# Rows without the norm's root, convolution taps of two tiles begun early, and another order of routing, in a two-layer decoder trunk

## The chip, the cores and the metric

The kernel runs on one core of a Trainium2 chip. The metric is the device time of one execution in microseconds (us), from 3 runs. A core has four engines for arithmetic, each with its own stream of instructions that runs strictly in the order written: TensorE (matrix products, PE in the rows), VectorE (DVE), ScalarE (ACT) and GpSimd (POOL). SyncE (SP) only starts transfers (DMAs) here. Engines wait for each other through semaphores. PSUM is the memory into which TensorE writes, 8 banks of 512 f32 for each of 128 partitions; SBUF is the memory of the others' tiles and of the weights.

## What is computed

272 rows (16 meta tokens ahead of 256) of 1024 values pass two layers, each a mixer and a feed-forward part, all in float32. The RMS norm stands ahead of each of the four; the diff touches the second and the third, and the routing of the fourth.

```python
def rms_norm(x, g):
    y = xf * lax.rsqrt(jnp.mean(xf * xf, axis=-1, keepdims=True) + EPS)
    return y * g

# layer 0: h = h + conv_sb_mixer(h); h = h + swiglu(rms_norm(h, ffn_norm_even), ...)
#   mixer: u = silu(layer_norm(causal_depthwise_conv(a * sigmoid(gate), width 31)))  (512 channels)
#          o = stick_breaking attention, 8 heads of 64; concat(u, o) @ w_out
def swiglu(x, w_gate, w_up, w_down):            # 1024 -> 2688 -> 1024
    return (jax.nn.silu(x @ w_gate) * (x @ w_up)) @ w_down

# layer 1, mixer (1408 channels)
    hcat = rms_norm(x, norm_g) @ w_in
    gate, xb = jnp.split(hcat, 2, axis=-1)
    gate = jax.nn.gelu(gate, approximate=True)
    xb = causal_depthwise_conv(xb, conv_w, conv_b)            # width 4
    # r, i = sigmoid(block-diagonal products of xb + bias)
    # a = exp(-8 r softplus(-lambda)); y_t = a y_(t-1) + sqrt(1 - a^2) i xb
    return (gate * y) @ w_out
# layer 1, experts: softmax over the top 2 of 8 logits, each expert a swiglu 1024 -> 3584 -> 1024
```

## The kernel before

**Layout.** Activations lie turned: channels on the partitions, the 272 rows along the free dimension, so `h` is 8 tiles (KD) of 128 x 272. The weights stream through in numbered *units* of 128 x 2048 f32 (1 MB; the last of a matrix may be smaller), and a unit is the step of the whole first part of the program: 0 to 3 the convolution's inputs (`U_CONV`), 4 to 9 q, k and v, 10 and 11 diagonal taps, 12 to 15 the even mixer's output (`U_OUT_E`), 16 to 37 the FFN's gate and up products in turn (`U_FFN1`), 38 to 49 its down projection (`U_FFN2`), 50 to 55 the odd mixer's input (`U_IN_O`), 56 to 61 its block-diagonal gates (`U_BAND`), 62 to 67 its gelu branch (`U_GELU`), 68 to 73 its output (`U_OUT_O`), and from 74 (`U_MOE`) on the experts, 84 units for each. The odd mixer has KL = 11 tiles of channels, in pairs with one alone at the end; its T of 272 columns are SEQ = 256 in the gelu branch.

**One product in three.** A float32 product is made of three at TensorE's rounded float32 (`three`, line 1529): each operand is split in a high part and the rest. For a weight unit ScalarE writes `whi` (line 639) and VectorE `raw_lo` = raw - `whi` (line 1010); the activations have pairs `hn_hi`/`hn_lo` (normalised rows), `hid_hi`/`hid_lo` (FFN), `xb_hi`/`xb_lo` (odd mixer). `raw` has 7 buffers, `whi` 6, and the experts' weights 14 (`MOE_RAW`).

**What sets the order.** ScalarE and VectorE each walk the units: split of unit u + 2 (u + 4 from `U_BAND` on, `AHEAD`), then `after(u)`, the work that hangs on unit u's products. So what VectorE does behind unit u stands behind the split of a later unit. TensorE's `features(u, ...)` does the products of unit u into PSUM banks `pair(u)` = 2 (u mod 3) and the next one.

**A norm** between two parts has this chain: VectorE adds the residual (line 1075 or 1099), ScalarE squares pairs of tiles (`square_pair`), TensorE sums the squares over the partitions with a product by ones (`norm_sums`, line 1552, bank 7), ScalarE takes the root as exp(-0.5 ln x) (`inverse_root`, into `rs`), then `norm_low` on VectorE and `norm_high` on ScalarE form h x gain x root, split, tile by tile. The next unit's first product needs the first tile, so TensorE waits for the whole chain after the last sums.

**FFN.** Behind each up unit ScalarE takes silu of the gate's bank (line 717), VectorE multiplies it by the up bank (`fh`, line 1087), ScalarE copies the high part and VectorE subtracts (line 1091). The down projection waits for the eleventh of these before its first product.

**Attention.** Heads go two at a time: scores, a log of 1 + exp, sums over later keys on TensorE, exp, product with v. Between VectorE's steps of it (`ll` line 1148, `zm` line 1176) stand the depthwise convolution's taps, `conv(n)` (line 1046), n at a time: tile by tile of `cacc`, each waiting for the tap before. Three of the four channel tiles (`CONV_PE`), 31 taps each, are done so; TensorE does the fourth, and parts of others, with diagonal matrices.

**Odd mixer.** Behind each input unit ScalarE writes the first tap from PSUM into `xc` (line 735), VectorE adds three more, again from PSUM (`lru_conv`, line 1239), and both split `xb`. Then ScalarE forms gates from `U_BAND`'s products. From `U_GELU` on VectorE scans (`scan(m)`, lines 1253 to 1258, the tiles of `SCAN_AT`), multiplies by the gelu (`gated`, line 1261) that ScalarE has made from PSUM (line 766), and subtracts the high part of the result (`y_low`, line 1265) that ScalarE copied (`y_high`). The gelu units' banks are `gelu_bank` = 0, 2, 4, 0, 2, 0, so the fourth unit may start once the first gelu is done, and the sixth once the fourth is. `turn_residual` brings `h` to the layout of rows in the first units of the input.

**Routing and experts.** TensorE gives the output in rows, VectorE adds `h_tok` in two halves (`acc`, line 1297), TensorE turns `acc` for the router's product (line 1777), the other two copy it out, VectorE picks the two best experts (`choose`), ScalarE sums the squares for the fourth norm, VectorE scales (`xs`, line 1321). The counts of earlier rows for each expert come from three small products, then rows are gathered with selection matrices `sel_m` (line 1806) and the experts follow. SyncE starts the experts' weight transfers in pieces of `over_gates_raw` (line 570), the first once the odd mixer's last low part stands, since they take the room of its tiles.

## Time and profile before

| | us |
|---|---|
| median of 3 runs | 1410.21 |
| lowest, highest | 1408.6, 1413.44 |
| the profiled execution's own time | 1408.68 |
| its span | 1406.7 |
| TensorE busy in it | 1334.8 (95%) |
| VectorE, ScalarE busy | 775.8 (55%), 639.3 (45%) |
| mean granted clock of TensorE | 0.977 |

TensorE's 95% is an average over two stages that differ. Up to some 540 us it works on the two layers' dense parts with other engines in turn; behind that the experts' weights come in at about 400 GB/s, and matrix products and transfers run side by side. Two lines of the page, busy share and transfers in 40 slices of 35 us, let the reader see the border at the sixteenth slice. The chain of work that ended last is 72% TensorE, 7% DMA, 5% VectorE and 4% ScalarE.

### The profile page before, as it was taken

The page shows a single profiled execution, that of the slowest core. Times are in us where ns is not written, and L with a number is a line of the kernel's source. Part 1 is how long each engine was busy: PE and PEld are TensorE (multiplying, and loading weights), DVE is VectorE, ACT ScalarE, POOL GpSimd, SP SyncE. Part 2 cuts the span into 40 slices and gives each one's busy share as a digit, 9 for nine tenths or more (in the row PEclk, how much of TensorE's full clock was granted, in tenths as well). Part 3 has the DMA queues.
Part 4 walks back from the last instruction along what each step waited for, and adds up shares of the span by engine and source line. Part 5 has one row for each costly group of instructions (what it writes and reads, how often), then busy time and mean ns, then how long its engine had stood idle before and what let it go on. Part 6 is the DMA issues. An engine that isn't in the chain of part 4 may idle for free.

```text
span 1406.7 us, 18570 instructions
## 1 busy us (share of the span) xinstructions
PE 1334.8 (95%) x7469; PEld 1011.3 (72%) x7469; DVE 775.8 (55%) x781; ACT 639.3 (45%) x581; POOL 19.1 (1%) x16
## 2 busy tenths in 40 slices
PE   6988889999999999999999999999999999999997
PEld 6977789999998978887336887345888335788433
DVE  5787455544476777994106984105995104987101
ACT  5453444433358756773006873005874004875100
POOL 0001000000002000000000000000000000000000
PEclk9997999999999998999999999999999999999999
DMA  9330245554526469998999999999999999999995
GB/s 329 105 106 30 65 141 170 156 167 158 182 90 189 165 234 385 364 363 326 396 410 409 412 409 410 391 408 411 412 407 412 412 407 412 412 406 413 406 406 234
DMA packets 149572, 426.34 MB, mean 303 GB/s; under 512 B 7664, under 2 KB 65648, under 8 KB 135152
## 3 DMA queue, kind: packets, MB, share of 16 engines
q1 hardware_dynamic: 149488, 425.12, 79.6%
q8 instruction: 65, 1.06, 0.3%
q14 instruction: 19, 0.16, 0.0%
HBM read 424.04 MB, written 1.05 MB: 302 GB/s over the span
## 4 chain that ended last, share of the span: by engine, by line
PE 72%; DMA 7%; DVE 5%; ACT 4%; issue 2%; SPq 1%; DVEq 0%; ACTq 0%
PE P L1529 51%; PE P L1919 12%; DMA over_gates_raw<-in_moe_w_gate 5%; PE P L1943 3%; PE P L1806 2%; DVE raw_lo L1010 1%; SPq L570 1%; DMA raw<-in_moe_w_down 1%; PE P L1827 1%; PE P L1861 1%; ACT whi L639 1%; ACT whi L867 1%; PE P L1552 0%; DVE over_gates_lo L1285 0%; PE P L1824 0%
## 5 line engine op out<-in xcount | busy, mean ns | idle before, releaser
L1529 PE MATMUL P<-hn_hi,whi 128*128 128x272 f32 (+1 forms) x640 | 187.6, 293 | 14.6 <-DVE hn_lo L1031 12.6
L1285 DVE TENSOR_TENSOR raw_lo<-raw,whi 128x2048 fp32r<-128x2048 f32 x84 | 189.3, 2287 | 10.7 <-ACT whi L867 10.1
L1529 PE MATMUL P<-hn_hi,raw_lo 128*128 128x272 f32 (+1 forms) x640 | 186.1, 291 | 0.0
L1529 PE MATMUL P<-whi,xe_hi 128*128 128x512 f32 x448 | 179.2, 400 | 7.1 <-DVE over_gates_lo L1285 7.1
L1529 PE MATMUL P<-hn_lo,whi 128*128 128x272 f32 (+1 forms) x640 | 185.7, 290 | 0.0
L867 ACT ACTIVATE whi<-raw 128x2048 fp32r<-128x2048 f32 x84 | 160.9, 1918 | 53.8 <-PE P L1529 33.0
L1010 DVE TENSOR_TENSOR raw_lo<-raw,whi 128x2048 fp32r<-128x2048 f32 (+3 forms) x72 | 149.9, 2105 | 53.7 <-ACT whi L639 53.7
L1529 PE MATMUL P<-whi,xe_lo 128*128 128x512 f32 x448 | 177.4, 396 | 0.0
L1285 DVE TENSOR_TENSOR over_gates_lo<-over_gates_raw,whi 128x2048 fp32r<-128x2048 f32 x72 | 162.9, 2287 | 19.4 <-ACT whi L867 18.8
L867 ACT ACTIVATE whi<-over_gates_raw 128x2048 fp32r<-128x2048 f32 x72 | 137.4, 1917 | 42.9 <-PE P L1529 17.3
L1529 PEld LDWEIGHTS P<-hn_hi,whi 128*128 128x128 f32 x640 | 122.5, 191 | 16.6 <-issue 13.8
L1504 DVE TENSOR_TENSOR hb<-silu,P 128x512 f32<-128x512 f32 (+1 forms) x16 | 9.9, 621 | 220.2 <-PE P L1919 220.2
L639 ACT ACTIVATE whi<-raw 128x2048 fp32r<-128x2048 f32 (+3 forms) x72 | 124.3, 1757 | 2.6 <-DMA raw<-in_w_in_even 2.6
L1529 PEld LDWEIGHTS P<-hn_lo,whi 128*128 128x128 f32 x640 | 123.0, 192 | 0.0
L1529 PEld LDWEIGHTS P<-hn_hi,raw_lo 128*128 128x128 f32 x640 | 122.7, 192 | 0.0
L1919 PE MATMUL P<-raw,xe_f 128*64 128x512 f32 (+1 forms) x576 | 114.8, 548 | 0.0
L1529 PEld LDWEIGHTS P<-whi,xe_hi 128*128 128x128 f32 x448 | 84.7, 189 | 31.4 <-DVE over_gates_lo L1285 11.3
L968 ACT ACTIVATE silu<-P 128x512 f32<-128x512 f32 (+1 forms) x16 | 8.7, 544 | 205.0 <-PE P L1919 205.0
L1529 PE MATMUL P<-raw_lo,xe_hi 128*128 128x512 f32 x256 | 101.2, 395 | 0.0
L1529 PEld LDWEIGHTS P<-whi,xe_lo 128*128 128x128 f32 x448 | 84.5, 189 | 19.1
L1529 PE MATMUL P<-whi,ht_lo 128*128 128x512 f32 x224 | 88.7, 396 | 0.0
L1529 PE MATMUL P<-whi,ht_hi 128*128 128x512 f32 x224 | 88.4, 395 | 0.0
(284 smaller groups left out, 2072.2 us busy)
## 6 DMA issues: line engine op xcount, KB each, us to landing
raw<-in_moe_w_up SPq DMA_DIRECT2D x64, 1024.0 KB, 15.1
raw<-in_moe_w_gate SPq DMA_DIRECT2D x64, 1024.0 KB, 15.2
over_gates_raw<-in_moe_w_down SPq DMA_DIRECT2D x64, 1024.0 KB, 16.6
over_gates_raw<-in_moe_w_gate SPq DMA_DIRECT2D x48, 1024.0 KB, 18.8
raw<-in_moe_w_down SPq DMA_DIRECT2D x40, 1024.0 KB, 15.5
over_gates_raw<-in_moe_w_up SPq DMA_DIRECT2D x32, 1024.0 KB, 16.3
over_xb_raw<-in_moe_w_up SPq DMA_DIRECT2D x16, 1024.0 KB, 15.2
raw<-in_w_in_even SPq DMA_DIRECT2D x10, 1024.0 KB, 10.6
```

Of the source, the lines that this page charges most:

```text
L570: sp.dma_start(moe_raw[k % MOE_RAW][:, :].rearrange("p (k m) -> p k m", k=kk), src)\
L639: act.activation(whi[u % HI][:, 0:w], raw[u % RAW][:, 0:w], ACT.Copy).then_inc(hi_ready, 1)
L867: act.activation(whi[u % HI][:, :], moe_raw[k % MOE_RAW][:, :], ACT.Copy).then_inc(hi_ready, 1)
L1010: dve.tensor_tensor(lo(u)[:, 0:w], raw[u % RAW][:, 0:w], whi[u % HI][:, 0:w].bitcast(F32), ALU.subtract).then_inc(lo_ready, 1)
L1285: dve.tensor_tensor(moe_lo(k), moe_raw[k % MOE_RAW][:, :], whi[u % HI][:, :].bitcast(F32), ALU.subtract).then_inc(lo_ready, 1)
L1504: dve.tensor_tensor(hb[:, 0:n], silu[:, 0:n], small_up(s), ALU.mult).then_inc(h_ready, 1)
L1529: last = pe.matmul(dst, lhs, rhs, start=start and n == 0, stop=stop and n == 2)
L1806: last = pe.matmul(P[:, 6 + k // 4, 128 * (k % 4):128 * (k % 4) + n], xs[:, c, 128 * k:128 * k + 128], sel_m[:, c, 0:n], start=c == 0, sto ...
L1827: last = pe.matmul(P[:, scatter_bank(n), :], sel_t[:, tokens], ys[:, 512 * half:512 * half + 512], start=True, stop=True)
L1861: last = pe.matmul(turn_banks(s)[:, 128 * n:128 * n + 128], tile_of(hb, n), cst("ident"), is_transpose=True, start=True, stop=True)
L1919: last = pe.matmul(dst[HALVES[b]], xe_f[:, k], w[:, at:at + half], start=k == 0, stop=k == KD - 1)
L1943: last = pe.matmul(P[HALVES[b], 4, :], ht_f[:, x:x + SMALL], w[:, at:at + 512], start=s == 0 and n == 0, stop=s == STEPS - 1 and n == tile ...
```

## The change

The diff has three parts.

**Convolution taps.** `conv` no longer goes through the taps of all three tiles in step, but by a list, `CONV_ORDER`: the first 12 taps of tiles 0 and 1 first, then the first 24 of tile 2 between the next 12 of both, then the rest. Eight taps are done behind each of units 1 to 3, ahead of q; behind each of the units from q on it is 10 (was 9), and between attention's steps 6 (was 10), as long as taps are left. `CONV_PER_UNIT` and `CONV_PER_PAIR` are the numbers.

**Rows without the root.** For the FFN and the odd mixer's input and gelu branch, `hn_hi`/`hn_lo` are now h x gain, without the root: ScalarE writes the high part and VectorE (`late_low`) the low part of each pair of tiles as soon as the residual is added. The sums of the last pair of squares are taken inside the first unit of the next part (`sums`), and the root (`late_root`) is formed while TensorE does that unit. The results are multiplied by the root, one factor per row (`by_token`): VectorE scales the gate's and the up's bank (`fgs`, `fh`) ahead of silu, the input's bank into a new tile `xn` from which the taps now read, and the gelu branch's bank into `gg` (`gelu_input`), where ScalarE takes the gelu in place. A bank is free once it is scaled. `gated` moves behind the two scans. The down projection waits for ten of the eleven parts of `hid`, in other banks (`down_bank`), and for the eleventh at its second group.

**Routing.** ScalarE's squares of each row block move ahead of copies, `choose(0)` moves behind the inverse, one of the splits of the experts' weights moves from ahead of the adds to ahead of the subtraction for the gathered rows, and the counts over all rows go to bank 5 with a signal of their own.

```diff
-CONV_PER_UNIT, CONV_PER_PAIR = 9, 10
+CONV_EARLY, CONV_PER_UNIT, CONV_PER_PAIR = 8, 10, 6
...
+CONV_ORDER = [(s, c) for s in range(12) for c in range(2)]
...
+CONV_ORDER += [(s, c) for s in range(24, CONV_W) for c in range(CONV_PE)]
...
+        def by_token(n, cols=slice(0, T)):
+
...
+        def down_bank(c):
+            return 2 * ((c + 2) % 3)
...
+                    for k in (2 * c, 2 * c + 1):
+                        last = act.activation(hn_hi[:, k], h[:, k], ACT.Copy, scale=v(NORMS[n], k))
+                    last.then_inc(nhi_ready, 1)
...
+            def late_root(n):
+
+                act.wait_ge(ss_ready, n + 1)
+                inverse_root(rs[:, 0], P[:, 7, 0:T], D, root_ready)
...
-                    act.wait_ge(unit_used, u)
+                    act.wait_ge(ffn_scaled, j + 1)
...
-                    act.activation(fsg[:, 0:n], P[:, pair(u - 1):pair(u - 1) + n, 0:T], ACT.Silu).then_inc(ffn_silu, 1)
...
-                    act.wait_ge(unit_used, u + 1)
+                    act.wait_ge(xn_ready, j + 1)
...
+                        act.wait_ge(gelu_scaled, g + 1)
+                        act.activation(gg[:, 2 * g:2 * g + n], gg[:, 2 * g:2 * g + n], ACT.Gelu_apprx_tanh)\
...
+            def squares(c):
+                act.wait_ge(h2_ready, c + 1)
...
+            squares(0)
             act.wait_ge(xt_done, 2)
             act.activation(*turned_copy(0, None), ACT.Copy).then_inc(xt_act, 1)
+            squares(1)
...
+                dve.wait_ge(nhi_ready, 4 * n + c + 1)
+                for k in (2 * c, 2 * c + 1):
+                    last = dve.scalar_tensor_tensor(out=hn_lo[:, k], in0=h[:, k], scalar=v(NORMS[n], k),
+                                                    in1=hn_hi[:, k].bitcast(F32), op0=ALU.mult, op1=ALU.subtract)
+                last.then_inc(norm_ready, 1)
...
-                    s, c = x // CONV_PE, x % CONV_PE
+                    s, c = CONV_ORDER[x]
...
+                    dve.wait_ge(uin_ready, c + 1)
+                    conv(CONV_EARLY)
+                elif u == 2:
+                    conv(CONV_EARLY)
...
+                    if u > U_OUT_E:
+                        late_low(1, u - U_OUT_E - 1)
...
                     dve.wait_ge(unit_used, u + 1)
...
+                    dve.tensor_tensor(fgs[:, 0:n], P[:, pair(u - 1):pair(u - 1) + n, 0:T], by_token(n), ALU.mult)\
+                        .then_inc(ffn_scaled, 1)
+                    dve.tensor_tensor(fh[:, 0:n], P[:, pair(u):pair(u) + n, 0:T], by_token(n), ALU.mult)\
+                        .then_inc(ffn_up, 1)
...
-                    if j >= 1:
-                        dve.wait_ge(ffn_lo, j)
...
+                    dve.tensor_tensor(fh[:, 0:n], fsg[:, 0:n], fh[:, 0:n], ALU.mult).then_inc(ffn_h, 1)
...
+                    if c >= 1:
+                        late_low(2, c - 1)
...
-                            gated(m)
+                        gelu_input(g)
...
+                    if 0 <= g < len(BAND_UNITS):
+                        for m in BAND_UNITS[g]:
+                            gated(m)
...
+                dve.wait_ge(unit_used, u + 1)
+                dve.wait_ge(root_ready, 3)
...
+                dve.tensor_tensor(xn[:, 0:n], P[:, xb_bank(j):xb_bank(j) + n, 0:T], by_token(n), ALU.mult)\
+                    .then_inc(xn_ready, 1)
...
-                        dve.scalar_tensor_tensor(out=xc[:, m, s:T], in0=P[:, xb_bank(j) + t, 0:T - s],
+                        dve.scalar_tensor_tensor(out=xc[:, m, s:T], in0=xn[:, t, 0:T - s],
...
+            def gelu_input(g):
+                n = min(2, KL - 2 * g)
+                dve.wait_ge(unit_used, U_GELU + g + 1)
...
+                dve.tensor_tensor(gg[:, 2 * g:2 * g + n], P[:, gelu_bank(g):gelu_bank(g) + n, 0:SEQ],
+                                  by_token(n, slice(META, T)), ALU.mult).then_inc(gelu_scaled, 1)
...
-            choose(0)
             dve.wait_ge(h2_sq, 2)
             inverse(st[:, 4:6], st[:, 0:2], D, h2_inv, 0)
+            choose(0)
...
+                dve.wait_ge(counted, 1)
+                step(dve.tensor_copy(count[:, :], P[:, 5, 0:NE]))
...
+            split_item_lo((0, 0), READY_LO - 2)
...
-            for k in range(READY_LO - 1, READY_LO):
-                split_item_lo((0, 0), k)
+            split_item_lo((0, 0), READY_LO - 1)
...
+                    if sums is not None and m == 0:
+                        norm_sums(sums, 3)
...
-            norm_sums(1, 3)
...
                     pe.wait_ge(ffn_h, (u - 3 - U_FFN1) // 2 + 1)
...
+                    pe.wait_ge(added_e, u - U_FFN1 + 2)
...
+                features(u, hn_hi, hn_lo, pair(u), norm=first, sums=first)
...
                 if u == U_FFN2:
+                    pe.wait_ge(ffn_h, (KF + 1) // 2 - 1)
+                if c == 1 and part == 0:
                     pe.wait_ge(ffn_h, (KF + 1) // 2)
...
-                features(u, hid_hi, hid_lo, 2 * (c % 3), k0=8 * part, start=part == 0, stop=part == 2)
+                features(u, hid_hi, hid_lo, down_bank(c), k0=8 * part, start=part == 0, stop=part == 2)
...
-            norm_sums(2, 3)
...
-                    pe.wait_ge(gelu_ready, n - 2 if n < 5 else 4)
+                    pe.wait_ge(gelu_scaled, n - 2 if n < 5 else 4)
...
+            pe.matmul(P[:, 4, NE:2 * NE], cst("tri_lt"), chosen[:, 1], start=False, stop=True).then_inc(slots_done, 1)
...
+            pe.matmul(P[:, 5, 0:NE], ones[:, :], chosen[:, 1], start=False, stop=True).then_inc(counted, 1)
```

What the three parts do to the order, at three places. First VectorE inside attention: `cacc` is the convolution's accumulator (its last number is the columns left after the shift), `ll` and `zm` are the steps of a pair of heads, `raw_lo` a split of weights. Before, from the second of two `ll`:

```order
L1148 SCALAR_TENSOR_TENSOR ll<-zm,lx 128x864 [waits zm_ready,ln_ready]
L1150 TENSOR_TENSOR ll<-ll,con 128x864 [waits dve_step]
L1046 SCALAR_TENSOR_TENSOR cacc<-uin,vec,cacc 128x251 [waits conv_step] x2
...
L1046 SCALAR_TENSOR_TENSOR cacc<-uin,vec,cacc 128x248 [waits conv_step] x2
L1010 TENSOR_TENSOR raw_lo_61<-raw_54,whi_63 128x2048 [waits hi_ready]
L1176 TENSOR_TENSOR zm<-P,zm 128x864 [waits r_done]
L1137 SCALAR_TENSOR_TENSOR zm<-P,con 128x432 [waits wexp_ready,z_done]
...
L1148 SCALAR_TENSOR_TENSOR ll<-zm,lx 128x864 [waits r_done,zm_ready,ln_ready]
...
L1046 SCALAR_TENSOR_TENSOR cacc<-uin,vec,cacc 128x247 [waits conv_step] x3
...
L1046 SCALAR_TENSOR_TENSOR cacc<-uin,vec,cacc 128x245 [waits conv_step] x3
L1176 TENSOR_TENSOR zm<-P,zm 128x864 [waits r_done]
```

After, from the last tap ahead of the first `ll` on:

```order
L1080 SCALAR_TENSOR_TENSOR cacc<-uin,vec,cacc 128x243 [waits conv_step] x3
L1194 SCALAR_TENSOR_TENSOR ll<-zm,lx 128x864 [waits zm_ready,ln_ready]
...
L1194 SCALAR_TENSOR_TENSOR ll<-zm,lx 128x864 [waits zm_ready,ln_ready]
...
L1080 SCALAR_TENSOR_TENSOR cacc<-uin,vec,cacc 128x242 [waits conv_step] x3
L1036 TENSOR_TENSOR raw_lo_61<-raw_54,whi_63 128x2048 [waits hi_ready]
L1222 TENSOR_TENSOR zm<-P,zm 128x864 [waits r_done]
L1183 SCALAR_TENSOR_TENSOR zm<-P,con 128x432 [waits wexp_ready,z_done]
...
L1194 SCALAR_TENSOR_TENSOR ll<-zm,lx 128x864 [waits r_done,zm_ready,ln_ready]
...
L1222 TENSOR_TENSOR zm<-P,zm 128x864 [waits r_done]
L1183 SCALAR_TENSOR_TENSOR zm<-P,con 128x432 [waits wexp_ready,z_done]
...
L1194 SCALAR_TENSOR_TENSOR ll<-zm,lx 128x864 [waits r_done,zm_ready,ln_ready]
```

The taps between the second `ll` and the first `zm` of the links (10) have become 3, and ahead of the next `zm` there are none; the tap list had got to its end.

Second, VectorE from the even output's last units to the first of the FFN: `h` is the residual add, `scr` the row times gain and root, `hn_lo` the low part of the row. Before:

```order
L1075 TENSOR_TENSOR h<-P,h 128x544 [waits unit_used]
L1010 TENSOR_TENSOR raw_lo_59<-raw_52,whi_68 128x2048 [waits hi_ready]
L1075 TENSOR_TENSOR h<-P,h 128x544 [waits unit_used]
L1025 SCALAR_TENSOR_TENSOR scr<-h,vec,rs 128x272 [waits root_ready,added_e]
...
L1031 TENSOR_TENSOR hn_lo<-scr,hn_hi 128x544 [waits nhi_ready,nf_ready]
...
L1010 TENSOR_TENSOR raw_lo_60<-raw_53,whi_63 128x2048 [waits hi_ready]
L1010 TENSOR_TENSOR raw_lo_61<-raw_54,whi_64 128x2048 [waits hi_ready]
L1087 TENSOR_TENSOR fh<-fsg,P 128x544 [waits ffn_silu,unit_used]
L1091 TENSOR_TENSOR hid_lo<-fh,hid_hi 128x544 [waits ffn_hi,ffn_h]
L1010 TENSOR_TENSOR raw_lo_62<-raw_55,whi_65 128x2048 [waits hi_ready]
```

After:

```order
L1036 TENSOR_TENSOR raw_lo_59<-raw_52,whi_68 128x2048 [waits hi_ready]
L1111 TENSOR_TENSOR h<-P,h 128x544 [waits unit_used]
L1064 SCALAR_TENSOR_TENSOR hn_lo<-h,vec,hn_hi 128x272 [waits nhi_ready]
...
L1064 SCALAR_TENSOR_TENSOR hn_lo<-h,vec,hn_hi 128x272 [waits nhi_ready]
...
L1036 TENSOR_TENSOR raw_lo_61<-raw_54,whi_64 128x2048 [waits hi_ready]
L1125 TENSOR_TENSOR fgs<-P,rs 128x544 [waits root_ready,unit_used]
L1127 TENSOR_TENSOR fh<-P,rs 128x544
L1131 TENSOR_TENSOR fh<-fsg,fh 128x544 [waits ffn_silu,ffn_up]
L1134 TENSOR_TENSOR hid_lo<-fh,hid_hi 128x544 [waits ffn_hi,ffn_h]
L1036 TENSOR_TENSOR raw_lo_62<-raw_55,whi_65 128x2048 [waits hi_ready]
```

The low parts stand behind each add and wait for ScalarE's high part alone, not for the root; the root is waited for by the first scaling, `fgs`.

Third, the gelu branch. VectorE before, one round (`tt<-tt,gg` is `gated`, `xb_lo` is `y_low`, the pieces between belong to the scans of two tiles):

```order
L1010 TENSOR_TENSOR raw_lo_61<-raw_54,whi_65 128x2048 [waits hi_ready]
L1261 TENSOR_TENSOR tt<-tt,gg 128x256 [waits gelu_ready,scanned] x2
L1265 TENSOR_TENSOR xb_lo<-tt,xb_hi 128x256 [waits y_hi_ready] x2
L1253 SCALAR_TENSOR_TENSOR tt<-rg,tt 128x272 [waits bscale_ready,decay_ready,xi_ready]
...
L1256 SCALAR_TENSOR_TENSOR tt<-rg,ig 128x272 [waits dve_step]
L1010 TENSOR_TENSOR raw_lo_62<-raw_55,whi_66 128x2048 [waits hi_ready]
```

After:

```order
L1036 TENSOR_TENSOR raw_lo_61<-raw_54,whi_65 128x2048 [waits hi_ready]
L1317 TENSOR_TENSOR gg<-P,rs 128x512 [waits unit_used]
L1327 TENSOR_TENSOR xb_lo<-tt,xb_hi 128x256 [waits y_hi_ready] x2
L1307 SCALAR_TENSOR_TENSOR tt<-rg,tt 128x272 [waits bscale_ready,decay_ready,xi_ready]
...
L1310 SCALAR_TENSOR_TENSOR tt<-rg,ig 128x272 [waits dve_step]
L1323 TENSOR_TENSOR tt<-tt,gg 128x256 [waits gelu_ready,scanned] x2
L1036 TENSOR_TENSOR raw_lo_62<-raw_55,whi_66 128x2048 [waits hi_ready]
```

And ScalarE there, after (before, the same places read `gg<-P` with a wait for `unit_used`):

```order
L789 ACTIVATE gg<-gg 128x512 [waits gelu_scaled]
L861 ACTIVATE xb_hi<-tt 128x256 [waits y_ready] x2
L656 ACTIVATE whi_65<-raw_54 128x2048 [waits raw_full5,unit_used]
L789 ACTIVATE gg<-gg 128x512 [waits gelu_scaled]
```

The scaling stands ahead of `y_low` in VectorE's round, and in ScalarE's the gelu of the scaled tile stands ahead of the high part that `y_low` waits for; `gated` comes a whole round of scans after the gelu.

## Rows read from the trace of the kernel before

**Rows 1.** Chain of waits in order of time (start us, length us, what)

```profile
663.72 7.02 PE P L1919 x32
...
750.69 11.38 PE P L1529 x48
...
966.96 11.36 PE P L1529 x48
```

**Rows 2.** The page's slices, what the transfers moved in each fortieth of the span

```profile
GB/s 329 105 106 30 65 141 170 156 167 158 182 90 189 165 234 385 364 363 326 396 410 409 412 409 410 391 408 411 412 407 412 412 407 412 412 406 413 406 406 234
```

**Rows 3.** Timeline (start us, length us, engine, line, operation, sizes, [idle before and releaser])

```profile
505.71 2.23 SPq L570 DMA_DIRECT2D over_gates_raw<-in_moe_w_gate  x4
...
520.03 2.35 DVE L1297 TENSOR_TENSOR acc<-P,h_tok 128x1024 f32<-128x1024 f32 x2
...
529.96 2.48 DVE L1321 SCALAR_TENSOR_TENSOR xs<-acc,st,gain 128x1024 f32<-128x1024 f32 x2
...
533.18 6.42 PE L1806 MATMUL P<-sel_m,xs 128*128 128x128 f32 x32 [1.21 <-DVE sel_m L1336]
```

**Rows 4.** Timeline of TensorE at the named holes

```profile
317.24 0.39 PE L1529 MATMUL P<-hid_hi,whi 128*128 128x272 f32 x1 [2.17 <-DVE fh L1087]
...
472.78 0.39 PE L1529 MATMUL P<-hn_hi,whi 128*128 128x256 f32 x1 [0.99 <-ACT gg L766]
...
521.39 3.48 PE L1777 MATMUL P<-con,acc 128*128 128x128 f32 x16 [3.00 <-DVE acc L1297]
```

**Rows 5.** Timeline of VectorE in attention

```profile
121.56 1.05 DVE L1176 TENSOR_TENSOR zm<-P,zm 128x864 f32<-128x864 f32 x1
...
130.41 3.52 DVE L1046 SCALAR_TENSOR_TENSOR cacc<-uin,vec,cacc 128x244 f32<-128x244 f32 x9
...
136.05 1.05 DVE L1176 TENSOR_TENSOR zm<-P,zm 128x864 f32<-128x864 f32 x1
```

**Rows 6.** The FFN's and the odd norm: two links of the chain, then the timeline

```profile
166.61 0.92 PE P L1552 x4
...
167.53 6.02 PE P L1529 x48
```

```profile
180.53 0.72 DVE L1075 TENSOR_TENSOR h<-P,h 128x544 f32<-128x544 f32 x1 [1.39 <-PE P L1529]
...
194.84 0.63 ACT L717 ACTIVATE fsg<-P 128x544 f32<-128x544 f32 x1 [0.25 <-PE P L1529]
...
383.60 0.72 DVE L1099 TENSOR_TENSOR h<-P,h 128x544 f32<-128x544 f32 x1 [7.83 <-PE P L1529]
...
398.68 1.05 ACT L735 ACTIVATE xc<-P,vec 128x272 f32<-128x272 f32 x2 [4.14 <-PE P L1529]
```

**Rows 7.** Timeline of VectorE, the eleventh part of the hidden rows

```profile
309.10 0.72 DVE L1087 TENSOR_TENSOR fh<-fsg,P 128x544 f32<-128x544 f32 x1 [7.27 <-PE P L1529]
```

**Rows 8.** Windows: us, busy PE PEld DVE ACT POOL, PEclk, DMA share, GB/s

```profile
105.00:110.00 5.00, 5.00 (x23) 4.87 (x22) 5.00 (x9) 0.00 (x0) 0.00 (x0) 0.50 0.00 0
...
390.00:398.00 8.00, 8.00 (x45) 7.95 (x46) 5.70 (x8) 3.11 (x3) 0.00 (x0) 0.67 0.00 0
```

**Rows 9.** Timeline of VectorE, taps of the odd mixer

```profile
425.58 2.52 DVE L1239 SCALAR_TENSOR_TENSOR xc<-P,vec,xc 128x271 f32<-128x271 f32 x6 [1.45 <-ACT xc L735]
...
430.32 1.56 DVE L1239 SCALAR_TENSOR_TENSOR xc<-P,vec,xc 128x271 f32<-128x271 f32 x3
```

**Rows 10.** Timeline of ScalarE and VectorE in the gelu branch

```profile
472.13 0.60 ACT L766 ACTIVATE gg<-P 128x512 f32<-128x512 f32 x1
...
473.55 0.75 DVE L1261 TENSOR_TENSOR tt<-tt,gg 128x256 f32<-128x256 f32 x2
...
482.98 2.27 DVE L1010 TENSOR_TENSOR raw_lo<-raw,whi 128x2048 fp32r<-128x2048 f32 x1
...
485.83 0.75 DVE L1265 TENSOR_TENSOR xb_lo<-tt,xb_hi 128x256 fp32r<-128x256 f32 x2
...
489.66 2.27 DVE L1010 TENSOR_TENSOR raw_lo<-raw,whi 128x2048 fp32r<-128x2048 f32 x1
```

97 lines of the change are left out of this document (53 added, 44 removed).

## Prediction

> **What bounds the kernel now.** I read the chain of waits in order of time first, then TensorE's own waits, then the other engines' rows around each of them. The end of the program is the expert stage: the second and the third pair of experts start 216.3 us apart (750.69 and 966.96 [rows 1]) while the transfers move some 410 GB/s in slice after slice [rows 2]. So the stage from 540 us on is a stream of weights at the transfers' rate, and no edit of the change touches it. What it can do is start earlier. Its start has two parts: the first expert transfer, which SyncE issues at 505.71 when the last low part of the odd mixer's result stands, and TensorE's first expert product, which follows the gather of 533.18 + 6.42 = 539.60 [rows 3]. The first 56 chunks (42 of the first expert and 14 of ring) need 56 x 2.57 us (216.3 / 84 chunks) = 144 us, so they would be in by 652 us; the first small expert begins at 663.72 [rows 1]. The transfers thus have some 12 us of slack against TensorE's start, and the end moves with TensorE's start as long as the first transfer does not fall back by more than that. Everything below is the shift of that start.
>
> Before it, TensorE is the bound, with named holes: 2.17 us ahead of the down projection, 0.99 in the gate products, 3.00 before the transposes of routing [rows 4], those inside attention, and the two norms.
>
> **Convolution taps.** 93 taps on VectorE, 39 of them inside attention, 10 ahead of each of three links of the chain and 9 ahead of the fourth. Now 24 run under the first input units (VectorE idles there) and 9 are left in attention: 6, then 3. A tap costs 3.52 / 9 = 0.39 us [rows 5]. One tap more ahead of attention costs 0.4. The first `ll` then starts 1.1 us earlier, TensorE's sums too; behind them stand 45 products of the diagonal taps, so the next link (121.56) gains only 2.4 us: TensorE is late there, no longer VectorE. The link at 136.05 loses its 9 taps as well: 2.4 + 3.4 = 5.8 us [rows 5]. All behind it hangs on it: **-5.8**, between -2.4 (if only TensorE's part counts) and -7.
>
> **FFN norm.** Unit 15 ends as VectorE adds at 180.53; the first FFN unit ends as ScalarE reads it at 194.84 [rows 6]: 14.3 us. A unit takes 6.02, a pair of norm sums 0.92. The rows without the root need only the add (0.72), ScalarE's two products (some 0.8) and VectorE's two (0.9): ready 2.5 us after the unit, while TensorE has 0.92 of sums and 2.3 of products of the first six tiles. So 0.92 + 6.02 + 0.92 = 7.9 with the last sums inside, and the root (Ln, Exp) has 12 us until the first scaling. 14.3 - 7.9 = 6.4; I take **-6.2**. Some 1.9 of it are the clock: that first unit took 7.9 us behind the wait, not 6.02. Low end -4.3.
>
> The price of the root comes back on every pair of FFN units: two more VectorE multiplies of 0.72 and a silu that can't begin before the up unit ends. From that end: scale gate, then silu beside scale up, multiply = 2.3 us to `ffn_h`, 2.9 to the high part; TensorE asks for the bank at 6.0. Cover: one unit. VectorE's load rises from 5.9 to 7.4 of 12 us. Nothing, unless the chain more than doubles.
>
> **Down projection.** It waited 2.17 us for `ffn_h` 11 behind two splits. It now asks for 10, in banks that are free. But its own low part is late: unit 35 ends at 309.10 [rows 7]; 2.9 us of chain, 1.9 of split by ScalarE, 2.3 by VectorE give 316.2 against 317.24: **-1.1**, from -2.2 to 0.
>
> **Odd norm and input.** 383.60 to 398.68 [rows 6] is 15.1 us; now 6.02 + 0.92 + some 0.35 waiting for the last pair = 7.3: -7.7, of which 2.7 is the clock (0.67 granted in 390 to 398 [rows 8]: the 1.2 GHz level for two thirds, after a wait). Then part is given back. Per unit VectorE now does split 2.2, scale 0.7, wait for ScalarE's first tap 0.45, `xb_lo` 0.7, six taps 2.44 = 6.5 us against TensorE's 6.02, and it starts 2 us late, since the split of unit 52 waits on ScalarE behind the root. Stepped through the six units, the last tap ends 35.2 us after the first unit where it was 33.2 (431.88 - 398.64) [rows 9]. ScalarE's gates hang on that, and its chain is the bound until the scans: +2.0. Together **-5.7**, between -7.7 and -3.7.
> A rule speaks for the better end: the Trainium skill (Perfetto Trace Analysis, Optimizing Scalar/DVE Operations) gives VectorE about 60 ns of overhead on SBUF and 125 on PSUM, and these taps now read `xn` in SBUF; an estimate by it is 33 x 0.065 = 2.1 us back, and a sum of -11.1. The rows show none of it: six taps from PSUM over 270 columns take 0.42 us each [rows 9], nine from SBUF over 243 take 0.39 [rows 5], and the 27 columns account for that. I stay with the rows.
>
> **Gelu and the output: the loss.** Here VectorE, not TensorE, is the chain: one round of 6.68 us (482.98 to 489.66) is split 2.2, `gated` 0.67, `y_low` 0.67, two scans 3.16 [rows 10]. The change puts the scaling (0.63 each, six of them) into it. Worse, the order: ScalarE's gelu waits for the scaling, the high part of y stands behind gelu on ScalarE, and VectorE's next instruction is the low part of it. From the scaling's start: 0.69, 0.5 of the gelu's 0.6 until ScalarE issues the next, 0.4, so `y_low` starts at 1.65 and not at 0.63: 1.02 us idle a round. Round: 8.33. TensorE's last gate unit needs the fourth scaling (it needed the fourth gelu, long done). From the same 471.36: first scaling at 473.55, second 479.1, third 487.5, fourth 495.8, done 496.5. TensorE has unit 65 from 474.3, 66 until 485.85, and starts 67 at 496.5 instead of 484.4 (472.78 [rows 4] and two units of 5.8): **+12.1** on all that follows. Its rows there are otherwise gapless, so nothing takes it back. The hole of 10.6 us also drops the clock; behind the norms' holes 1.9 and 2.7 were lost, I take **+2**. The first transfer moves by +8.2 only, so the slack holds. Ends: +6 (were the idle hidden and the clock kept) and +19.
>
> **Routing.** VectorE adds `acc` at 520.03, 1.6 us after TensorE's end, behind the third split; that split moves, and the first half is added before that end, so the transposes start 3.0 us earlier. The squares (2 x 1.2) move ahead of the copies, the copies of row block 1 end 3.9 us after TensorE's end (was 6.3), the two choices follow the root, and `xs` (2.48) [rows 3] ends at 9.8 instead of 14.05; gather at 10.5 instead of 14.8: **-4.3**, between -7 (with the gather at full clock, 3.5 instead of 6.42) and -2. Counting in bank 5 is off the path.
>
> **Sum**: -5.8 - 6.2 - 1.1 - 5.7 + 12.1 + 2 - 4.3 = **-9.0 us**. The profiled run took 1408.68 (span 1406.7 plus 2.0), the median is 1410.21: 1399.7 or 1401.2, I say 1400.5.
>
> **Rivals.**
> 1. The gelu round costs only its instructions (ScalarE's order hides the idle, the clock holds): 3 x 1.02 + 2 less, -14, so 1396. For it: ScalarE has time to spare there, 0.6 us of gelu a round. Against: the order is strict on both engines. 0.12.
> 2. The holes cost more and attention gives less: the low clock lasts as long as behind the hole before 101.48, where it still was 0.50 in 105 to 110 [rows 8], some 10 us, 5 lost instead of 2, and attention only -2.4: -2.6, 1407.5, no difference. 0.13.
> 3. The clock part of the norms does not come back, the low level falls elsewhere: without 1.9, 2.7 and 2 the sum is -6.4, so 1404. Beside it stands the Trainium skill (TensorE: Matmul & The Clock Gate, Part 1), which puts the ramp under 1% of a typical span and advises against fitting it; 0.05, the rows [rows 8] show it.
> 4. Slower: behind the 10.6 us hole TensorE stays at the low level through the output products. 132 products at 0.235 are 31 us, as much again if all are at half rate: -9.0 - 2 + 31 = +20, 1430. It decides from 22 us at the low level on. Against: behind the norm's hole it came back under work, inside 390 to 398. 0.04.
>
> **How the numbers follow.** Forecast 0.66 (1396.5 to 1405), rivals as given. A measurement of this kernel tells 0.3% (4.2 us) from nothing: faster needs under 1406. Faster 0.66 + 0.12 + 0.05, less 0.01 for the forecast's own tail: 0.82; same 0.13 + 0.01; slower 0.04. The range takes in rivals 1 to 3 and the worse ends of attention and odd input: 1393 to 1408.
>
> **What would show it.** After's TensorE waits: none over 0.5 us at either norm, about 1 at the down projection, about 10 before one gate unit on the gelu scaling; the first FFN unit in 6 us; the clock low right behind that hole; the first expert product at about 530.5 and the first transfer at about 495. It is wrong if the last gate unit waits under 5 us, if FFN units wait at all, or if the first expert product moves and the end does not.

## The result and the profile after

The changed kernel takes 1398.92 us (median of 5 runs, 1393.68 to 1402.48), the kernel before 1411.84 over the five runs that stand beside them: a ratio on record of 0.9919, with an interval of 0.9898 to 0.9940 (the quotient of the two medians is 0.9909). The forecast was 1400.5, between 1393 and 1408. The span of the profiled execution went from 1406.7 to 1397.1 us, by 9.6, where the sum on record had 9.0.

Two sums that agree prove little: five of the seven terms hold within 0.5 us, two are off by 1.8 and 1.6 us in opposite directions, and one of the five, the routing, has its size only beside another term. The rows first.

The experts' stage, from the chain of waits (start us, us, what), as [rows 1]:

```profile
530.23 22.23 PE P L1592 x96
...
741.23 11.36 PE P L1592 x48
...
957.30 11.36 PE P L1592 x48
```

The pairs still stand 216.1 us apart, and each of these starts is 9.4 to 9.7 us earlier than its like in [rows 1] and the gather's end in [rows 3]. So the stage is moved as a whole and, but for 0.3 us, not changed, and everything that the change did lies ahead of 530 us.

Attention and the norms, VectorE's timeline (start us, us, engine, line, operation, sizes, and in brackets the idle time before and its releaser), as [rows 5, 6]:

```profile
105.95 1.05 DVE L1222 TENSOR_TENSOR zm<-P,zm 128x864 f32<-128x864 f32 x1
...
117.62 1.06 DVE L1222 TENSOR_TENSOR zm<-P,zm 128x864 f32<-128x864 f32 x1 [3.36 <-PE P L1696]
...
128.66 1.05 DVE L1222 TENSOR_TENSOR zm<-P,zm 128x864 f32<-128x864 f32 x1
...
172.96 0.72 DVE L1111 TENSOR_TENSOR h<-P,h 128x544 f32<-128x544 f32 x1 [0.56 <-PE P L1592]
...
186.83 0.73 DVE L1125 TENSOR_TENSOR fgs<-P,rs 128x544 f32<-128x544 f32 x1 [1.74 <-PE P L1592]
...
368.61 0.72 DVE L1142 TENSOR_TENSOR h<-P,h 128x544 f32<-128x544 f32 x1 [7.00 <-PE P L1592]
...
378.26 0.71 DVE L1282 TENSOR_TENSOR xn<-P,rs 128x544 f32<-128x544 f32 x1
```

VectorE now waits 3.36 us for TensorE ahead of the second of these `zm`: TensorE is the later one there, as the prediction put it. The sizes are larger than forecast: this link comes 3.9 us earlier than its like (121.56 in [rows 5]) and not 2.4, the next one 7.4 and not 5.8. From the last residual add to the end of the second FFN unit it takes 186.83 - 172.96 = 13.9 us instead of 20.3. The last row has no idle time before it: VectorE came to the odd mixer's first scaling late, from a split.

TensorE's holes, its timeline, as [rows 4]:

```profile
302.29 0.36 PE L1592 MATMUL P<-hid_hi,whi 128*128 128x272 f32 x1 [1.25 <-DVE raw_lo L1036]
...
477.47 0.58 PE L1592 MATMUL P<-hn_hi,whi 128*128 128x256 f32 x1 [10.60 <-DVE gg L1317]
...
482.08 0.39 PE L1592 MATMUL P<-whi,xb_hi 128*128 128x512 f32 x1
...
512.46 0.40 PE L1592 MATMUL P<-raw_lo,xb_hi 128*128 128x512 f32 x1
```

The holes at the two norms are gone, and the one that was forecast with 10.6 us ahead of the last gate unit is there with 10.60. That unit takes 482.08 - 477.47 = 4.6 us where 24 products at 0.119 are 2.9: the clock granted in it is 0.59. One round of the gelu branch on VectorE and ScalarE, as [rows 10]:

```profile
459.99 0.68 DVE L1317 TENSOR_TENSOR gg<-P,rs 128x512 f32<-128x512 f32 x1
...
460.71 0.63 ACT L789 ACTIVATE gg<-gg 128x512 f32<-128x512 f32 x1 [3.96 <-DVE gg L1317]
461.25 0.71 ACT L861 ACTIVATE xb_hi<-tt 128x256 fp32r<-128x256 f32 x2
...
461.68 0.76 DVE L1327 TENSOR_TENSOR xb_lo<-tt,xb_hi 128x256 fp32r<-128x256 f32 x2 [1.00 <-ACT xb_hi L861]
...
468.37 0.68 DVE L1317 TENSOR_TENSOR gg<-P,rs 128x512 f32<-128x512 f32 x1
...
476.74 0.68 DVE L1317 TENSOR_TENSOR gg<-P,rs 128x512 f32<-128x512 f32 x1
```

The scaling at 459.99 releases the gelu at 460.71, behind it stands the high part at 461.25, and only that lets VectorE go on at 461.68, after 1.00 us of idle time. The round is 8.37 us (8.33 on record). And the start of routing, SyncE, ScalarE and TensorE:

```profile
497.09 2.20 SPq L587 DMA_DIRECT2D over_gates_raw<-in_moe_w_gate  x4
...
509.85 1.92 ACT L890 ACTIVATE whi<-over_gates_raw 128x2048 fp32r<-128x2048 f32 x1 [0.64 <-DMA over_gates_raw<-in_moe_w_gate]
511.78 1.28 ACT L900 ACT_TABLE_LOAD   x1
513.07 1.06 ACT L903 ACTIVATE sq<-acc 128x1024 f32<-128x1024 f32 x1
...
524.07 1.20 PE L1877 MATMUL P<-sel_m,xs 128*128 128x128 f32 x4 [1.22 <-DVE sel_m L1398]
```

The prediction did not look at this chain. ScalarE's first square (513.07, for the fourth norm) stands behind its fourth split of an expert piece (509.85), which waited for the fourth landing of the transfers that start at 497.09 (the forecast had them start at about 495). TensorE ends the output at 512.46 + 0.40 = 512.86, so ScalarE gets free 0.2 us after it. The two nearly coincide.

### The profile page after: what moved, and what is told of

The parts are those of the page before. It is cut to its first block, busy times and chain, and to the rows that moved or that the text cites. A ratio compares the mean times of both kernels' runs of the same rounds, so it can differ in the third digit from the quotient of the medians.

```text
span 1397.1 us, 18640 instructions
## 1 busy us (share of the span) xinstructions
PE 1330.4 (95%) x7469; PEld 1007.4 (72%) x7469; DVE 792.5 (57%) x807; ACT 642.6 (46%) x589; POOL 18.1 (1%) x16
## 3 DMA queue, kind: packets, MB, share of 16 engines
HBM read 424.04 MB, written 1.05 MB: 304 GB/s over the span
## 4 chain that ended last, share of the span: by engine, by line
PE 77%; DMA 7%; DVE 6%; ACT 5%; issue 3%; SPq 2%; DVEq 0%; ACTq 0%
PE P L1592 55%; PE P L1990 12%; DMA over_gates_raw<-in_moe_w_gate 5%; PE P L2014 3%; PE P L1877 2%; SPq L587 2%; DVE raw_lo L1036 1%; DMA raw<-in_moe_w_down 1%; ACT whi L656 1%; PE P L1898 1%; PE P L1932 1%; DVE xc L1293 1%; PE P L1696 1%; ACT whi L890 1%; DMA raw<-in_w_in_even 1%
## 6 DMA issues: line engine op xcount, KB each, us to landing
raw<-in_w_in_even SPq DMA_DIRECT2D x10, 1024.0 KB, 10.5
```

## Experiments

**How they are read.** Where a stage is at issue, I count from the first scan of the odd mixer (the first `TENSOR_TENSOR_SCAN` of VectorE: 467.58 before, 448.49 after), since what lies ahead of it varied among these profiled executions by up to 6 us at the same order of taps (below) and has nothing to do with an edit behind it. In us behind the first scan:

| | output's end | first expert transfer | gather's end | second pair |
|---|---|---|---|---|
| before | 50.8 | 38.1 | 72.0 | 283.1 |
| after | 64.4 | 48.6 | 81.8 | 292.7 |
| g1, high part first | 63.1 | 44.1 | 79.1 | 290.8 |
| g2, no scaling | 52.0 | 38.2 | 75.3 | 285.3 |
| g3, GpSimd scales | 57.2 | 45.7 | 82.3 | 293.4 |
| g4, hole filled | 62.7 | 48.6 | 81.8 | 292.6 |
| r1, routing alone | 50.8 | 38.1 | 73.0 | 283.4 |
| s1, g2 with splits later | 52.0 | 38.1 | 70.8 | 281.3 |
| h2, split ahead of the root | 64.3 | 48.6 | 81.7 | 292.8 |
| k3, copied, splits later | 57.6 | 44.1 | 74.8 | 285.1 |
| k1, k3 and h2 | 59.0 | 44.1 | 75.5 | 286.2 |
| k4, k1 with copies ahead | 53.2 | 44.1 | 71.9 | 282.9 |
| c1, taps undone | 65.3 | 48.6 | 81.5 | 292.4 |
| f1, FFN norm undone | 64.3 | 48.6 | 81.8 | 292.7 |

The change as a whole costs 9.6 us in this part (292.7 against 283.1), where the terms on record for gelu, clock and routing add up to +9.8. Each row is one profiled execution.

### The gelu branch

**g1.** ScalarE's high part ahead of the gelu.

```diff
                     g = u - U_GELU
+                    if g >= 1:
+                        for m in BAND_UNITS[g - 1]:
+                            y_high(m)
                     if u < U_OUT_O:
...
-                    if g >= 1:
-                        for m in BAND_UNITS[g - 1]:
-                            y_high(m)
```

> The changed kernel with ScalarE's high part of y ahead of the gelu in each round of the gelu branch; nothing else is altered. My theory: the changed kernel's VectorE stands idle 1.00 us ahead of the low part in each round, since ScalarE does the gelu first; two of these stand ahead of the fourth scaling, which the last gate unit waits for. So that unit's wait goes from 10.6 to 8.6 us, the round from 8.37 to 7.35, and the kernel from 1398.9 to 1396.9. Rival (the round costs only its instructions, the order on ScalarE hides): no idle to take away, wait 10.6, 1398.9.

Measured 1398.79 us (4 runs), no difference to the changed kernel; against before 0.9909 (0.9889 to 0.9930). In the trace the theory's steps are there: no idle time ahead of the low part, a round of 7.28 us, and

```profile
477.83 0.58 PE L1592 MATMUL P<-hn_hi,whi 128*128 128x256 f32 x1 [8.43 <-DVE gg L1317]
```

The wait is 2.2 us shorter, so the idle time is real and held the fourth scaling. What it is worth is less clean: the output's end comes 1.3 us earlier behind the first scan, the second pair 1.9, and the edit also moved the first expert transfer forward by 4.5 us, so that ScalarE is ready for the routing ahead of TensorE (it waits 3.01 us for `acc`). The median shows no gain.

**g2.** The multiplication by the root left out of the gelu branch, so the result is another one: `gelu_input` is not called, ScalarE's gelu reads `P` after `unit_used`, and TensorE's three waits are for `gelu_ready`.

> The changed kernel with the multiplication of the gelu branch's results by the root left out: ScalarE takes the gelu straight from PSUM as before, and TensorE waits for the gelu, not for the scaling (the result is then not the reference's; all else computes as in the changed kernel). My theory: the scaling in VectorE's round is what holds the last gate unit. Without it the unit does not wait, its first wait for a bank shrinks by 1.5 us, the clock stays up (1.75 us), so the output's first product moves from 482.08 to some 468, and the kernel from 1398.9 to 1385. Rival (TensorE would wait for something else there, the scans or the splits): the wait keeps over 5 us and the kernel stays over 1392.

Measured 1392.09 (ratio 0.9875, 0.9840 to 0.9909): 6.8 us under the changed kernel and not 14. The output does end 12.4 us earlier, so the scaling holds TensorE as my theory says. But the gather's end gains 6.4 and the second pair 7.4. ScalarE and TensorE of g2:

```profile
497.79 1.91 ACT L892 ACTIVATE whi<-over_gates_raw 128x2048 fp32r<-128x2048 f32 x1 [2.01 <-DMA over_gates_raw<-in_moe_w_gate]
499.72 1.28 ACT L902 ACT_TABLE_LOAD   x1
501.02 1.06 ACT L905 ACTIVATE sq<-acc 128x1024 f32<-128x1024 f32 x1
...
503.37 6.97 PE L1859 MATMUL P<-router_g,xnt 128*128 128x8 f32 x32 [3.48 <-ACT xnt L910]
```

TensorE has ended the output at 497.48, ScalarE's fourth split begins at 497.79, waiting for a landing, and the first square comes 3.5 us after the output's end. The router's 32 products wait 3.48 us for it. This is a bound that is not on record. And the wait costs a second time: behind it these products take 6.97 us, at a granted clock of 0.50, where in the changed kernel, after a wait of 0.16 us, they take 3.92:

```profile
515.43 3.92 PE L1859 MATMUL P<-router_g,xnt 128*128 128x8 f32 x32 [0.16 <-ACT xnt L908]
```

Wait (3.3 us more) and products (3.05 more), less 0.4 in the gather, are the 6.0 us between the output's 12.4 and the gather's 6.4.

**g3.** The scaling given to GpSimd: ScalarE copies the bank to `gg`, GpSimd multiplies it there by the root, ScalarE's gelu follows behind `y_high`; TensorE waits for the copies.

> The changed kernel with the gelu branch's results copied out of PSUM by ScalarE (which frees the bank), multiplied by the root in SBUF by GpSimd, which is idle there, and then the gelu in place behind the high part of y. Everything is computed. My theory: VectorE's round is 6.7 us again, ScalarE has room for six copies of 0.6 us, so nearly the whole 14 us of the scaling come back: 1385. Rival (two engines on SBUF at once: six GpSimd multiplications of some 1.2 us slow VectorE for as long): 7 us less gained, 1392.

Measured 1401.58 (0.9923, 0.9896 to 0.9951): neither. The output does end 7.2 us earlier behind the first scan than in the changed kernel (57.2 against 64.4), but the gather ends no earlier (82.3 against 81.8). GpSimd, VectorE and TensorE of g3:

```profile
454.58 3.41 POOL L641 TENSOR_TENSOR gg<-gg,rs 128x512 f32<-128x512 f32 x1 [11.23 <-ACT gg L798]
...
456.75 1.53 DVE L1318 SCALAR_TENSOR_TENSOR tt<-rg,tt 128x272 f32<-128x272 f32 x1
...
466.48 1.38 DVE L1320 TENSOR_TENSOR ig<-ig,tt 128x272 f32<-128x272 f32 x1
...
472.58 0.58 PE L1603 MATMUL P<-hn_hi,whi 128*128 128x256 f32 x1 [6.16 <-ACT gg L798]
```

In each round one or two of VectorE's operations last 1.4 to 1.7 us instead of 0.4 to 0.7, while GpSimd's multiplication (1.3 to 1.5 us) runs. The Trainium skill (Perfetto Trace Analysis, Optimizing Scalar/DVE Operations) says that the two engines share an SBUF read port, so that moving work between them may not help; the trace agrees, by some 1 us a round. And TensorE still waits 6.16 us, now for ScalarE's fourth copy, since ScalarE itself stood in the round before, at the gelu and at `y_high`. The 7.2 us that did arrive at the output's end were lost in the routing, as in g2: ScalarE's four splits again, a first square 5.7 us behind the output's end, and router products that wait 4.31 us and then take 6.96:

```profile
516.09 6.96 PE L1870 MATMUL P<-router_g,xnt 128*128 128x8 f32 x32 [4.31 <-ACT xnt L921]
```

**g4.** 84 products of 256 columns into bank 6 in the hole.

```diff
+                    if n == 5:
+                        for f in range(84):
+                            pe.matmul(P[:, 6, 0:SEQ], hn_hi[:, f % KD, 0:128], hn_hi[:, 0, META:T], start=True, stop=True)
                     pe.wait_ge(gelu_scaled, n - 2 if n < 5 else 4)
```

> The changed kernel with 84 products of 256 columns into an unused bank put into TensorE's hole ahead of the last gate unit (10.6 us; they take 84 x 0.12 = 10.0 us). My theory: the clock falls because TensorE stands idle there; with the products it stays at the full level, the unit takes 2.9 us and not 4.6, and the kernel goes from 1398.9 to 1397.2. Rival (the low level behind the hole comes from elsewhere or falls later): the unit still takes over 4 us, or the products behind it do, and the time stays 1398.9.

Measured 1400.25 (0.9925, 0.9899 to 0.9952). The unit runs at the full level and the output ends 62.7 us behind the first scan instead of 64.4: 1.7 us, so the term for the clock (2 us) is confirmed. Nothing of it arrives: the gather ends at 81.8 in both. The trace shows ScalarE's splits again: the first square stands at 512.52, 1.9 us behind the output's end, and the router's products now wait 1.84 us, where in the changed kernel it was 0.16.

### Who holds the routing

**r1.** The kernel before with the third part of the diff.

> The kernel before with the routing part of the change alone. The prediction on record prices it at 4.3 us and lets the end move with TensorE's first expert product: 1406.1 against 1410.4. New theory: ScalarE stands behind its four splits of the first expert pieces, whose transfers start only after the last low part of y; in the kernel before it gets free at 521.65 (split to 520.35, then 1.28 of table load), 3.3 us after TensorE's end of the output (518.39), while in the changed kernel the two nearly fall together (513.06 and 512.86). From ScalarE's first square to the gather it is 11.0 us in the changed kernel, so here the gather starts at 532.7 instead of 533.2: 0.5 us, 1409.9.

Measured 1412.02 over 10 runs, before 1411.35 over 25: a ratio of 1.0011 (0.9997 to 1.0026). The routing part, on record with -4.3 us, gives no gain in the kernel before. ScalarE and TensorE of r1:

```profile
518.91 1.91 ACT L867 ACTIVATE whi<-over_gates_raw 128x2048 fp32r<-128x2048 f32 x1 [0.64 <-DMA over_gates_raw<-in_moe_w_gate]
520.85 1.28 ACT L877 ACT_TABLE_LOAD   x1
522.14 1.06 ACT L880 ACTIVATE sq<-acc 128x1024 f32<-128x1024 f32 x1
...
524.49 6.14 PE L1791 MATMUL P<-router_g,xnt 128*128 128x8 f32 x32 [3.04 <-ACT xnt L885]
```

The same picture as in g2: first square at 522.14, the output's end at 518.77, a wait of 3.04. My figure here was 0.5 us of gain, it came out as 1.0 us of loss at the gather's end. The router's products do start 0.5 us earlier behind the first scan (56.5 against 57.1). But in the kernel before, they took

```profile
524.66 3.80 PE L1787 MATMUL P<-router_g,xnt 128*128 128x8 f32 x32
```

and here, behind the wait of 3.04 us, 6.14, at a granted clock of 0.65 in their first half and 0.50 in the second, where it was 0.95. That is 2.3 us lost, of which the gather gave 0.8 back (5.58 us instead of 6.42).

**s1.** g2 with one split each on ScalarE and VectorE ahead of the routing, instead of four and two.

```diff
-            for k in range(4):
+            for k in range(1):
                 split_item_hi(0, k)
...
-            for k in range(4, READY):
+            for k in range(1, READY):
...
-            for k in range(READY_LO - 2):
+            for k in range(READY_LO - 3):
...
-            split_item_lo((0, 0), READY_LO - 2)
+            for k in range(READY_LO - 3, READY_LO - 1):
+                split_item_lo((0, 0), k)
```

> The kernel g2 (root's multiplication in the gelu branch left out, so that its result is not the reference's) and beside it only one instead of four of ScalarE's splits of expert pieces, and one instead of two of VectorE's, ahead of the routing; the others follow behind the root and during the gather. New theory: in g2 TensorE's output ended 15.4 us earlier than in the changed kernel but the first expert product only 9.4, since ScalarE still waited for the transfers of its four splits. With one, the routing starts with the output's end again, 17.2 us to the first expert product instead of 23.1: 1392.1 - 5.9 = 1386.2. Rival (the experts' stage starts with its transfers, and these do not move): 1392.

Measured 1390.47 (0.9847, 0.9823 to 0.9871). Of the 5.9 us the gather's end shows 4.5 and the second pair 4.0; ScalarE now waits 5.5 us for `acc` ahead of its first square, no longer the other way round. The run moves splits of both engines at once. It was ScalarE's that held: VectorE's second ended at 495.54 in g2, 1.9 us ahead of the output's end, and VectorE then waited for TensorE. The median gained 1.6. Attention alone moved the profiled executions of the two by 5.6 us (first residual add at 155.70 in s1, at 150.11 in g2), so medians of four runs can't price this. The shift behind the first scan can, and r1 and g4 point the same way.

### The two parts that gain

**c1.** The taps as before: `CONV_ORDER` in step, numbers 0, 9 and 10.

> The changed kernel with the taps of the convolution in the order and the numbers of before (all three tiles in step, none behind units 1 to 3, 9 a unit, 10 between attention's steps). Five executions of the changed order now have the first residual add of the even output at 150.1 to 155.6 us (middle 153.1), the kernel before had it at 160.6. My theory now: the taps were the chain in attention, and undoing them costs 7.5 us: 1406.4, the add near 160.6. The prediction on record says 5.8: 1404.7. Rival (TensorE was the chain there and the taps only fill): below 3 us, so under 1402.

**f1.** The FFN's norm as before.

> The changed kernel with the FFN's norm as before: the root multiplied into the rows, sums of the last pair ahead of the first unit, silu from PSUM, one multiplication a pair of units. Down projection, odd mixer and routing stay as changed. My theory: from the last add to the end of the second FFN unit it takes 20.3 us as before instead of 13.9, all of it reaches the end: 1398.9 + 6.4 = 1405.3. Rival (the two more multiplications a pair delay something behind, so part comes back when they go): 3 us or less, under 1402.

c1 measured 1407.53 over 10 runs, 8.6 us over the changed kernel (against before 0.9976, 0.9963 to 0.9990); f1 measured 1405.64 over 10 runs, 6.7 over it (0.9959, 0.9942 to 0.9975). The changed kernel's five runs are from another session, where the kernel before was 0.5 us slower. Both rivals fall. In f1 it takes 20.8 us from the last add (175.73) to the end of the second unit (196.56).

c1 gives more than the 5.8 on record, and the other runs show why. Of the fourteen profiled executions three have attention with the old taps and eleven with the new ones. Windows over 100 to 112 us (length, busy time of PE, PEld, DVE, ACT and POOL, then granted clock, DMA share, GB/s), of the kernel before, of g1, of the changed kernel and of g2:

```profile
100.00:112.00 12.00, 10.52 (x43) 10.08 (x44) 10.87 (x17) 2.74 (x3) 0.35 (x1) 0.57 0.12 43
...
100.00:112.00 12.00, 10.60 (x45) 10.14 (x45) 8.95 (x11) 5.06 (x5) 1.92 (x1) 0.57 0.22 75
...
100.00:112.00 12.00, 11.66 (x66) 11.43 (x67) 7.84 (x10) 5.94 (x6) 2.05 (x1) 0.72 0.15 50
...
100.00:112.00 12.00, 11.46 (x85) 10.92 (x86) 8.04 (x10) 5.94 (x6) 2.03 (x1) 1.00 0.26 71
```

| taps | executions | clock granted in 100 to 112 us | first residual add |
|---|---|---|---|
| old | before, c1, r1 | 0.57 to 0.60 | 160.6 to 161.3 |
| new | g1, g3, f1, s1, k4 | 0.57 | 154.8 to 155.8 |
| new | after, g4, k3 | 0.72 | 152.5 to 153.1 |
| new | g2, h2, k1 | 1.00 | 149.4 to 150.1 |

At equal clock the taps give 160.95 - 155.45 = 5.5 us (means of the first two lines), close to the 5.8 of the step. On top of that TensorE's wait for `ll` at some 100 us is 1.84 us instead of 3.17, and behind it the clock fell later or not at all in six of eleven executions, for up to 5.7 us more. These eleven are eleven kernels, each profiled once; their edits all lie behind attention, and what decides the clock in one execution and not in the other, no run here tells.

### The odd mixer, and a faster kernel

**h2.** `split_hi(u + 3)` ahead of `late_root` on ScalarE, at both norms.

> The changed kernel with ScalarE's split of the next weight unit (1.9 us) moved ahead of each of the two late roots, for whose sums ScalarE waits 2.4 us anyway. The odd input stage gave 4.1 us and not 5.7, and I put that down to the first scaling: it starts at 378.26, some 2.2 us after the unit's end, behind VectorE's split, which waits for ScalarE's, which stands behind the root. My theory: the first scaling then follows the unit's end, and of the 2.2 us 1.5 to 2.2 arrive at the first scan (TensorE's own pace takes over behind): 1397.1 against 1398.9. Rival (VectorE's load of 6.6 us a unit is what counts, so it falls back to the same place): 0, 1398.9.

Measured 1400.68 (0.9927, 0.9899 to 0.9955), no gain. The first scaling does come 7.7 us behind the last add instead of 9.65 (365.27 and 372.96; after: 368.61 and 378.26), so the split was what held it. At the last tap 1.05 of the 1.96 us were left, and at the first scan nothing (VectorE and TensorE of h2):

```profile
372.96 0.72 DVE L1284 TENSOR_TENSOR xn<-P,rs 128x544 f32<-128x544 f32 x1 [1.32 <-PE P L1594]
...
413.85 0.59 PE L1594 MATMUL P<-xb_hi,whi 128*128 128x272 f32 x1 [3.68 <-ACT ig L777]
```

Behind this wait of 3.68 us TensorE's product took 0.59 us; the same one in the changed kernel, after the same wait, 0.39. It is the clock: over the next 6.2 us 0.51 of it was granted, in the changed kernel 0.72. Here that took back 1.1 us that k1, with the same edit, kept up to the first scan.

**k3, k1, k4** leave nothing out. k3: ScalarE copies the gelu's bank to SBUF, VectorE scales it there, the gelu stands behind `y_high`, TensorE waits for the copies, and the splits are those of s1. k1 adds h2. k4 makes each copy one round earlier:

```diff
+                        for x in ((0, 1) if g == 0 else (g + 1,) if g + 1 < len(BAND_UNITS) else ()):
+                            w = min(2, KL - 2 * x)
+                            act.wait_ge(unit_used, U_GELU + x + 1)
+                            act.activation(gg[:, 2 * x:2 * x + w], P[:, gelu_bank(x):gelu_bank(x) + w, 0:SEQ],
+                                           ACT.Copy).then_inc(gelu_copied, 1)
```

> The changed kernel with the gelu branch copied out of PSUM by ScalarE (bank free then), scaled in SBUF by VectorE, the gelu behind y's high part, and one split of an expert piece on ScalarE and on VectorE ahead of the routing instead of four and two. All is computed. My theory: TensorE's last gate unit no longer waits (its output ends 52 us behind the first scan, as in g2, and not 64.4); the first transfer comes 44.1 us behind it, as in g1, and no longer holds the routing. First expert product 70.6 us behind the first scan (81.5 in the changed kernel): 1398.9 - 10.9 = 1388.0. Rival (with the start earlier than the transfers allow, the stream takes some of it: 56 chunks x 2.57 = 144 us from a first transfer 26.5 us ahead of the first product, when the kernel before had 33.7): 5 us of it lost, 1393.

> The kernel k3 with ScalarE's splits ahead of the late roots as in h2. Everything is computed. Theory: both gains add, 1388.0 - 1.8 = 1386.2, a ratio of 0.982 to the kernel before. Rival: the gain of the earlier split is lost in the odd mixer, 1388.

> The kernel k1 with each of ScalarE's copies out of PSUM in the gelu branch one round earlier (two in the first round), ahead of the gelu that waits for VectorE. Everything is computed. In k1 and k3 the last gate unit still waited 6.9 us, now for the fourth copy, which stood behind the third gelu and so behind VectorE's round again. My theory: with the copy a round earlier there is no wait; the output ends 52 us behind the first scan and not 59.0, the first product of the experts comes at 69 and not 75.3: 1392.1 - 6 = 1386. Rival (the first transfer, still 44 us behind the first scan, now starts only 25 us ahead of the experts' first product, so the stream is the bound and the end stays): the second pair starts no earlier than in k1 (286.2 us behind the first scan), 1391 to 1392.

Measured: k3 1389.90 (0.9852, 0.9822 to 0.9881), k1 1392.14 (0.9863, 0.9841 to 0.9885), k4 1391.00 (0.9852, 0.9830 to 0.9875). All three are 1.4 to 1.5% faster than the kernel before and 7 to 9 us faster than the changed one; among themselves they can't be told apart. The expectations were 1388.0, 1386.2 and 1386: k3 came within 2 us, k1 and k4 missed by 6 and 5. TensorE in k3, and in k4:

```profile
470.98 0.58 PE L1597 MATMUL P<-hn_hi,whi 128*128 128x256 f32 x1 [6.87 <-ACT gg L791]
```

```profile
476.35 0.50 PE L1601 MATMUL P<-whi,xb_hi 128*128 128x512 f32 x1 [1.42 <-DVE raw_lo L1046]
```

I had missed in k3 that ScalarE's fourth copy stands behind its third gelu, and so behind VectorE's round: 6.87 us. In k1 the earlier split did bring the first scan 1.1 us nearer to the first residual add than in k3, but the output ended 1.4 us and the second pair came 1.1 us later behind that scan. The clock shows why. Windows over the 6 us from the last gate unit's start, of k3 and of k1, after waits of 6.87 and 6.85 us:

```profile
470.98:476.98 6.00, 6.00 (x32) 5.70 (x33) 5.90 (x11) 2.44 (x4) 0.00 (x0) 0.73 0.07 25
```

```profile
466.19:472.19 6.00, 6.00 (x26) 5.90 (x27) 5.90 (x11) 2.44 (x4) 0.00 (x0) 0.50 0.01 3
```

k4 takes that wait away, and TensorE then meets the next one, VectorE's splits of the output's weights, twice 1.4 us; the output takes 34.2 us where it takes 30.8 in the changed kernel. Behind the first scan k4 is 3.3 us ahead of k1, half of what I expected. Its median, 1391.00, is the rival's number, but the rival's mechanism fell: the first transfer is 27.8 us ahead of the gather's end, instead of 33.9 in the kernel before, and the second pair, which the rival had no earlier than k1's, still comes 211 us behind the gather, as in every run here (210.0 to 211.6). The stream of weights has that much slack.

## Why the prediction was right, and where not

| term | on record | measured, us |
|---|---|---|
| attention | -5.8 | -7.6 (180.53 to 172.96) |
| FFN norm | -6.2 | -6.5 (20.3 to 13.9) |
| down projection | -1.1 | -0.9 (317.24 to 302.29, less 14.0) |
| odd norm and input | -5.7 | -4.1 (first scan 467.58 to 448.49, less 15.0) |
| gelu, output | +12.1 | +11.8 (13.6 at the output's end, less 1.8 of clock) |
| clock behind the hole | +2 | +1.8; 1.7 in g4 |
| routing | -4.3 | -3.8 here; no gain in the kernel before |
| sum | -9.0 | -9.4 at the gather's end, -9.6 in the span |

The measured figures are differences of two profiled executions. Taps, FFN norm and routing also have runs of their own (c1, f1, r1); the down projection and the odd norm have none.

**Attention.** The mechanism and its size hold at equal clock (5.5). The step that failed is the upper bound: "-7" left no room for what comes on top when the clock falls later behind the shorter hole, 1.8 us here. Rival 2 priced the clock only as a loss.

**FFN and down projection.** As worked out. The changed kernel's chain of waits has the first FFN unit with the sums inside: 3.02 us of products from 173.84 on, 0.92 of sums, and the rest without a wait. The multiplies by the root cost nothing on the path: no FFN unit waits.

**Odd norm and input.** That "it starts 2 us late, since the split of unit 52 waits on ScalarE behind the root" was right, h2 shows it; the six units then took 33.8 us from the first scaling to the last tap, and the last tap was 35.8 us behind the first unit's end, not 35.2; the unit itself ended 7.7 us behind the last add and not 7.3, and the gates lost 0.75 more. Together some 1.6 us, inside the bounds. By the Trainium skill (Perfetto Trace Analysis, Optimizing Scalar/DVE Operations), with its lower overhead for operands in SBUF than in PSUM, the estimate on record was 2.1 us back here. The trace disagrees: six taps from `xn` in SBUF take 2.55 us, those from PSUM took 2.52 [rows 9].

```profile
380.24 2.55 DVE L1293 SCALAR_TENSOR_TENSOR xc<-xn,vec,xc 128x271 f32<-128x271 f32 x6 [1.26 <-ACT xc L760]
```

**Gelu.** Foreseen with its mechanism, its place and its size; g1 shows the idle time, g2 the hole, g4 the clock. Rival 1's price was wrong, though: it counts three idle times, but two stand ahead of the fourth scaling (461.68 and its like a round later), as in the sum's own steps, so it should have been 4 us and not 5. And the first transfer moved by 10.5 us behind the first scan, not by 8.2.

**Routing.** This is the step that failed, though its number looks right. "The transfers thus have some 12 us of slack against TensorE's start" holds for the stream as far as it was tried: k4 used 6 us of it. But the first four pieces have another reader: ScalarE splits them ahead of the squares, and its fourth landing ends some 13 us after the first transfer starts. In the kernel before that chain ends 3.3 us after TensorE, so a faster routing behind TensorE finds ScalarE late (r1), and TensorE, having waited, then does the router's products at the lower clock. The prediction priced neither. In the changed kernel the gelu hole delays TensorE by 13.6 us and the first transfer by 10.5, which brings the two level, and there the 3.8 us arrive. That they arrive only because of the hole is concluded from r1 and g2; no run takes the routing part out of the changed kernel. Seen so, the hole cost less than the 13.6 us: without it (g2) the gather gains 6.4.

**Rivals.** Rival 2 needed attention at -2.4, which fell. Rival 1 (the round hides its idle time) fell with the 1.00 us in each round. Rival 3 (the norms' clock does not come back) fell with 6.5 at the FFN. Rival 4 (the low level lasts through the output) fell: it lasted 16 products (0.21 us apart, then 0.12). The 9.6 us came from the forecast's own case, with two terms off by 1.8 and 1.6 us in opposite directions; that the total lies 0.6 us from the sum is in part luck.

## What to carry to other kernels

When a transfer is said to have slack, list every reader of its first pieces, not the last consumer alone: an engine that prepares them in its strict order can hold work that has nothing to do with them. And price what TensorE does behind a wait at the lower clock: in r1, g2 and g3 waits of 3.0 to 4.3 us cost another 2.3 to 3.1. An edit's worth depends on which of two chains is late at its place, so a part that gains in a bundle can be worth nothing alone; run it alone. And stages are compared from a common event inside the trace, since a few microseconds of another stage's clock hide what an edit does.

## What the runs showed of the hardware

Eleven kernels that are the same up to attention's end, with the same wait of 1.84 to 1.86 us ahead of the same product, were granted a mean clock of 0.57, 0.72 or 1.00 over 100 to 112 us, and the first residual add of the even output came at 155, 153 or 150 us accordingly. With a wait of 3.17 or 3.18 us, in the three kernels with the old taps, it was 0.57 to 0.60. The Trainium skill (TensorE: Matmul & The Clock Gate, Part 1) calls the ramp run-variable and under 1% of a typical span. Both are compatible with the rows, but 6 us of 1400, or 0.4%, is as much as one of this change's terms.

TensorE's 32 small products for the router, 128 x 8 each, took 3.80 us with no wait ahead (before) and 3.92 after one of 0.16 (after), but 6.14, 6.97 and 6.96 after waits of 3.04, 3.48 and 4.31 us (r1, g2, g3), at a granted clock of 0.50 throughout in g2 and g3 and in the second half in r1. After one of 1.84 us (g4) it was 4.27. A wait is not the only thing that counts: in s1 they took 5.11 with none right ahead.

GpSimd's multiplication of 128 x 512 with a broadcast operand took 1.3 to 1.5 us in the middle of the branch, but 3.41 at its first; the last, of 128 x 256, took 3.89. Beside one, an operation of VectorE lasted some 1 us longer.
